# A stride of 8224 bytes for the split-weight slots of a two-layer decoder trunk

## What is computed

```python
def swiglu(h, w_gate, w_up, w_down):
    return (jax.nn.silu(h @ w_gate) * (h @ w_up)) @ w_down

def moe_swiglu(h, w_router, w_gate, w_up, w_down):
    ...
    top_logit, top_idx = lax.top_k(logits, TOP_K)      # TOP_K = 2 of N_EXPERTS = 8
    gates = jax.nn.softmax(top_logit, axis=-1)
    ...
    ys = lax.map(run, (xs, block_expert)).reshape(L, D)   # run: swiglu with this expert's weights
    out = jnp.zeros((T, D), h.dtype).at[rows_token].add(ys * rows_gate[:, None])
```

## Time and profile before

| what | value |
|---|---|
| median of 2 runs | 1575.46 us (1573.89 to 1577.03) |
| the profiled execution | 1580.12 us |
| its span, first to last instruction | 1578.3 us |
| mean granted TensorE clock over the span | 0.947 |
| weights moved, all DMA | 428.34 MB |

### The profile page before, as it was taken

One profiled execution on the slowest core, in us unless ns is written; L12 is line 12 of the kernel. 1 busy time (PEld: TensorE's weight loads), 2 busy tenths in 40 slices (PEclk: granted clock), 3 DMA queues, 4 the chain that ended last, 5 costly groups with the idle time before them and its releaser, 6 DMA issues.

```text
span 1578.3 us, 19914 instructions
## 1 busy us (share of the span) xinstructions
PE 1492.4 (95%) x7534; PEld 1257.3 (80%) x7534; DVE 1154.7 (73%) x959; ACT 957.9 (61%) x868; POOL 7.9 (1%) x18
## 2 busy tenths in 40 slices
PE   4997999999978879999999999999999999999996
PEld 4995689998765668888888888888888888888885
DVE  3454454545557469879979978987987987987985
ACT  3553244434445367768677767768677767766773
POOL 1000000000000000000000000000000000000000
PEclk8995799999985779999999999999999999999999
DMA  9561144555512139999999998997997998998990
GB/s 291 184 212 54 54 163 171 183 200 186 178 54 81 50 129 378 396 338 331 393 343 333 394 382 292 394 383 288 387 394 290 385 395 292 381 395 298 373 395 33
DMA packets 201923, 428.34 MB, mean 271 GB/s; under 512 B 8848, under 2 KB 42672, under 8 KB 201872
## 3 DMA queue, kind: packets, MB, share of 16 engines
q1 hardware_dynamic: 200736, 424.18, 73.6%
q0 software_dynamic: 1136, 3.47, 0.9%
HBM read 426.57 MB, written 1.05 MB: 271 GB/s over the span
## 4 chain that ended last, share of the span: by engine, by line
PE 89%; DVE 5%; ACT 3%; issue 1%; DMA 1%; SPq 0%; DVEq 0%; ACTq 0%
PE ps L1142 27%; PE ps L1144 27%; PE ps L1143 27%; PE ps L1438 2%; PE ps L1482 2%; DVE w_lo L684 1%; PE ps L1286 1%; DMA raw<-in_w_mem_kv_dram 1%; PE ps L1168 1%; PE ps L1261 1%; ACT w_hi L397 0%; PE ps L1339 0%; PE ps L1461 0%; DVE small L741 0%; PE ps L1462 0%
## 5 line engine op out<-in xcount | busy, mean ns | idle before, releaser
L1065 DVE TENSOR_TENSOR e_wlo<-raw,e_whi 128x2048 fp32r<-128x2048 f32 x336 | 750.9, 2288 | 94.0 <-ACT e_whi L620 94.0
L620 ACT ACTIVATE e_whi<-raw 128x2048 fp32r<-128x2048 f32 x336 | 620.2, 1918 | 39.4 <-PE ps L1144 39.3
L1142 PE MATMUL ps<-e_whi,act_hi 128*128 128x512 f32 x1344 | 528.5, 393 | 3.4 <-DVE act_lo L1078 1.9
L1144 PE MATMUL ps<-e_wlo,act_hi 128*128 128x512 f32 x1344 | 523.8, 390 | 0.0
L1143 PE MATMUL ps<-e_whi,act_lo 128*128 128x512 f32 x1344 | 523.2, 389 | 0.0
L1142 PEld LDWEIGHTS ps<-e_whi,act_hi 128*128 128x128 f32 x1344 | 252.4, 188 | 56.5 <-issue 3.1
L1144 PEld LDWEIGHTS ps<-e_wlo,act_hi 128*128 128x128 f32 x1344 | 252.3, 188 | 53.4
L1143 PEld LDWEIGHTS ps<-e_whi,act_lo 128*128 128x128 f32 x1344 | 252.5, 188 | 50.9
L684 DVE TENSOR_TENSOR w_lo<-raw,w_hi 128x2048 fp32r<-128x2048 f32 (+2 forms) x68 | 148.5, 2198 | 160.4 <-ACT w_hi L397 160.3
L397 ACT ACTIVATE w_hi<-raw 128x2048 fp32r<-128x2048 f32 (+2 forms) x68 | 124.1, 1840 | 107.4 <-PE ps L1144 91.0
L1142 PE MATMUL ps<-act_hi,w_hi 128*128 128x256 f32 (+3 forms) x480 | 137.6, 287 | 14.0 <-DVE act_lo L697 14.0
(11 more groups left out here) (203 smaller groups left out, 1134.6 us busy)
## 6 DMA issues: line engine op xcount, KB each, us to landing
raw<-in_w_exp_gate_dram SPq DMA_DIRECT2D x112, 1024.0 KB, 7.6
raw<-in_w_exp_up_dram SPq DMA_DIRECT2D x112, 1024.0 KB, 8.0
raw<-in_w_exp_down_dram SPq DMA_DIRECT2D x112, 1024.0 KB, 8.5
raw<-in_w_dense_gate_dram SPq DMA_DIRECT2D x11, 1024.0 KB, 5.1
raw<-in_w_dense_up_dram SPq DMA_DIRECT2D x11, 1024.0 KB, 5.2
raw<-in_w_dense_down_dram SPq DMA_DIRECT2D x11, 1024.0 KB, 5.5
raw<-in_w_out_dram SPq DMA_DIRECT2D x8, 1024.0 KB, 5.0
raw<-in_w_in_a_dram SPq DMA_DIRECT2D x7, 1024.0 KB, 6.8
```

What stands on the lines that cost most here:

```text
L620: nc.scalar.activation(e_whi[:, (s - NPRE) % E_SPLIT, :], raw[:, s % RAW, :], ACT.Copy)\
L1065: nc.vector.tensor_tensor(e_wlo[:, r, :], raw[:, s % RAW, :], e_whi[:, r, :].bitcast(F32), ALU.subtract).then_inc(lo_ready, 1)
L1142: nc.tensor.matmul(dst, l_hi, r_hi, start=start, stop=False)
L1144: return nc.tensor.matmul(dst, l_hi, r_lo, start=False, stop=stop)
```

## The change

The six slots before the experts become one tensor `w_split`, the twelve of the experts one tensor `e_split`, each with rows of 2048 + 8 float32, that is 8224 bytes. The old names are views of these tensors, and a slot still uses its first 2048 elements.

```diff
+STAGGER = 8
...
-            w_hi = sbp("w_hi", [P, SPLIT, SLOT], F32R)
-            w_lo = sbp("w_lo", [P, SPLIT, SLOT], F32R)
+            w_split = sbp("w_split", [P, 2 * SPLIT, SLOT + STAGGER], F32R)
+            w_hi, w_lo = w_split[:, 0:SPLIT, 0:SLOT], w_split[:, SPLIT:2 * SPLIT, 0:SLOT]
...
-        e_whi = sb("e_whi", [P, E_SPLIT, SLOT], F32R)
-        e_wlo = sb("e_wlo", [P, E_SPLIT, SLOT], F32R)
+        e_split = sb("e_split", [P, 2 * E_SPLIT, SLOT + STAGGER], F32R)
+        e_whi, e_wlo = e_split[:, 0:E_SPLIT, 0:SLOT], e_split[:, E_SPLIT:2 * E_SPLIT, 0:SLOT]
```

## The result

The changed kernel takes 1592.59 us (1592.46 to 1592.71, 2 runs) against 1575.46; the ratio is 1.011, 95% interval 1.0086 to 1.0134. That is 17 us, clear of noise, inside the predicted range and inside 2%, but not the "no change" that the prediction held likeliest.

The account below looks back on a forecast made before the run. TensorE's matmul pace was taken to bound the kernel. All terms were taken as zero: 1580.12 + 0 us for the profiled execution, against the median 1575.46 + 0, rounded to 1576 us, range 1548 to 1627.

Parts of the forecast that it names:

- What bounds the kernel: Experts: time is the sum of TensorE's own steps, transfers and splits ahead; a change is worth its effect on matmul pace.
- The likeliest case, zero: Whole kernel: the moved operands leave the matmul pace unchanged, 1576 us; chance 0.43 for no change within 10 us.
- the bounds: 5528 moved matmuls: from -74 us, the whole handover gone, to +50 us, the pace right behind the transposes.
- Rows 9: Dense down, stationary operand 256 and 768 bytes past a multiple of 1024: 15 matmuls at 0.2267 us each, so price zero.
- rows 7: An expert's timeline before, stationary operand at 0: 25 matmuls of 512 columns at 0.2264 us each.
- rows 10: Gate slots: 24 matmuls with 96 stationary columns at multiples of 256 take 115.8 ns each, the next 24, 128 bytes past, 120.0.
- the dearer level may be a ceiling that the others already pay: A 128-column operand at a multiple of 256 already takes 120 ns, so moved matmuls might pay nothing more.
- The misaligned operand costs: Rival: every moved matmul pays the gate slots' 4.2 ns, 5528 in all, +23 us, 1599 us; chance 0.18 around there.
- The gate slots: Before the experts: halves at 115.8 and 120.0 ns should move together if the address, not the output half, made the difference.
- The two reads part: Rival: stagger separates weight load and moving read, 11 ns on 5528 matmuls, -61 us, 1515 us; chance 0.09, in part 0.12.
- VectorE, ScalarE and DMA unchanged: Experts: subtractions stay at 2288 ns, copies at 1918 ns, and no transfer changes because `raw` stays.
- 3584 matmuls move, 448 keep their price: Experts: of 4032 matmuls only those reading hi slot 0 in two of three products keep their addresses.

Follow-up runs that it names:

- the chains: Kernels with the trunk left out, only chains of 48 or 72 products as in `three` at given operand offsets; 226.7 ns a matmul at 0, 0 with 512 columns.
- the first kernel of chains: Trunk left out, only chains of 48 products at given operand offsets, other engines idle; 512 columns took 226.7 ns each at 0, 0 and 233.5 at 32, 0.

## Why the prediction was right, and where not

*What bounds the kernel*: right. The loss is the pace of TensorE times the count of matmuls; a pace 4.5 ns slower in 4032 matmuls is 18 us, and nothing hid any of it.

*The range, 1548 to 1627 us*: the time lies in it because it was made wide enough for the rivals, not because the likeliest case was right. And 31.5 us is not the least change that can be told from none: 10 runs of the kernel with everything shifted against 13 of the one before give a ratio to 0.1%.

*The likeliest case, zero*: wrong. The step that failed is the choice between the bounds, with the sentence that zero "is the row that it is nearest to". Rows 9 had the stationary operand 256 and 768 bytes off, which are distance 0 in a period of 256; together with rows 7 they were one point, not two, and could say nothing of 32. The row off the period was rows 10 alone, and I set it aside for its width. Its 4.2 ns are nearly the 4.5 that the experts show, but that closeness is luck: in the chains, 128 bytes cost 3 ns with 96 stationary and 256 moving columns and 5.6 with 128 and 512. That "the dearer level may be a ceiling that the others already pay" held in the chains with 256 columns (at 120 ns no distance is dearer by much) and not with 512.

*The misaligned operand costs, 1599 us*: this rival came true in its size, measured 1592.6. Its condition was off. It is not the operand's own address, as the kernel with everything shifted by 32 bytes shows (1575.42 us), but the distance to the other one. The experts lost more than its sum gave them, 18 us against 3584 x 4.2 = 15, and the 8 us for the 1944 matmuls before them are not in the time (1576.14 us with that half alone): the 512-column ones there lose about 3 us, and with 256 columns an offset is mostly a small gain. The gate slots show it as foretold; their halves, at 67.40, 70.22 and 73.05 us after, have moved together to 2.82 and 2.83 us, 117.5 and 117.9 ns.

```profile
67.40 0.28 PE L1143 MATMUL ps<-act_hi,w_split 128*96 128x256 f32 x1
...
70.22 0.28 PE L1143 MATMUL ps<-act_hi,w_split 128*96 128x256 f32 x1
...
73.05 0.28 PE L1143 MATMUL ps<-act_hi,w_split 128*96 128x256 f32 x1
```

*The two reads part, 1515 us*: wrong. With 512 columns no distance of those tried brings a gain, and the 13 ns at the handover stay in every one; no run shows the 11 ns of its sum. With 256 columns part of them does come back, 2.2 ns in most cases and 6.7 in the best (113.3 against 120.0). The Trainium skill's page "TensorE: Matmul & The Clock Gate", section "Step-by-step: what each phase is for", has the weight load on a read port of its own that takes nothing from the running matmul. The chains do not agree that the two are independent: with the stationary operand at 32 in both, the pace is 226.9 ns when the moving one is at 32 and 233.1 when it is at 0. Whether it is the read of the weights that disturbs the stream they do not show.

*VectorE, ScalarE and DMA unchanged*: right, 2284 ns, 1918 ns and the same bytes. *3584 matmuls move, 448 keep their price*: by distance, the 224 matmuls that read lo slot 2 keep theirs too, since it begins 256 bytes past a multiple of 1024. But the count is too fine, since a matmul's cost hangs on its neighbours as well: a chain of the first kernel of chains with the offsets of slot 0 (moving hi 0, lo 192, stationary 0; L116, 190.14 to 201.15) took 229.4 ns on average. And the pace settles: L108 of that kernel, at distance 256 behind a chain at 128, takes 10.93 us (102.05 to 112.98, the next start) against 10.88; its first 12 matmuls take 230.8 ns each, its last 226.7. The same is seen in L114, at (64, 64) behind (32, 32), where the distance stays 0 and only the place changes: 10.91 us.

Still open is what in the chip makes the distance matter. The runs show, for 512 columns, a period of 256 bytes, a level of 226.7 ns at distance 0, and 2 to 10 ns more elsewhere, unevenly. They do not show the mechanism.

## What to carry to other kernels

Where TensorE is the bound and moves 512 columns of fp32r against 128 stationary columns, with a weight load for each matmul, keep the start of the moving and of the stationary operand at the same place within 256 bytes of the partition: 3% of the pace hung on it here. Shift both, or shift by multiples of 256, and nothing is lost. A run with one stage changed that comes out even may hold a loss and a gain: here the stage before the experts had both, and only the pace by width showed it. And when a trace has no row for a new address, ask in which period it would count before calling an old row near: 256 and 768 were no evidence for 32.

## What the runs showed that I had not expected

- TensorE's pace depends on where its two operands in SBUF lie to each other: 226.7 ns at distance 0, 233.5 at 32, 229.2 at 64, 232.3 at 128 bytes, with nothing else running on the core.
- The sign counts: the moving operand 64 bytes ahead takes 228.9 ns, 64 behind 233.3.
- At 256 moving and 128 stationary columns the order turns round, 120.0 ns at distance 0 and 117.8 or 113.3 with the stationary operand at 64; with 96 stationary columns it does not (116.7 at 0, 119.6 at 128).
- The pace settles over a chain: behind a chain with other offsets, distance 0 can need several matmuls to reach 226.7 ns (the first 12 of L108 took 230.8 each).
